# Delta-rule heads on raw keys and queries, decay rows loaded by broadcast, and a fourth weight chunk kept at the end

## The reference, cut to what matters

```
qkv = silu(_dwconv_centred(concat([g_q, g_k, g_v]), gdn_conv_w))       # 5 taps
gq = _l2norm(heads(gq)) * GDN_DK ** -0.5                               # t * rsqrt(sum(t*t) + RMS_EPS)
gk = _l2norm(heads(gk))
gc = cumsum(g, axis=-1)                                                # log decays within a chunk
decay = exp(where(tril, gc[..., :, None] - gc[..., None, :], -inf))
kb = k * beta[..., None]
a = where(strict, kb @ k^T * decay, 0.0) + eye
sol = triangular_solve(a, concat([v * beta, kb * exp(gc)]))            # u, w
attn = q @ k^T * decay;  q_dec = q * exp(gc);  k_dec = k * exp(gc[-1] - gc)
# over the chunks: v_new = u - w @ state;  o = q_dec @ state + attn @ v_new
#                  state = state * exp(gc[-1]) + k_dec^T @ v_new
o = o_f + o_b                                                          # both directions
o = o * rsqrt(mean(o * o) + RMS_EPS) * gdn_norm_w * silu(heads(g_z))
```

## Time and profile before

| what | value |
|---|---|
| median of 3 runs | 1485.69 us (1484.23 to 1486.91) |
| the profiled execution's own time | 1485.09 us |
| its span, first to last instruction | 1483.3 us, mean granted TensorE clock 0.990 |
| TensorE busy | 1417.9 us, 96% |
| VectorE, GpSimd, ScalarE busy | 796.2, 485.3, 462.3 us |
| attention ends, head 0 begins | about 242 us |
| heads 0 to 3 begin their Q projection | 248.7, 350.5, 452.4, 554.2 us |
| the output projection begins | 646.1 us |

### The profile page before, as it was taken

How to read it: one execution, slowest core, us unless ns; L and a number is a source line. 1 busy time by engine, 2 the same in 40 slices (tenths; PEclk the granted TensorE clock), 3 DMA queues, 4 the chain that set the end, 5 groups by cost and what they waited for, 6 DMA issues and landing times.

```text
span 1483.3 us, 19658 instructions
## 1 busy us (share of the span) xinstructions
PE 1417.9 (96%) x7102; PEld 1163.3 (78%) x7102; DVE 796.2 (54%) x1360; ACT 462.3 (31%) x875; POOL 485.3 (33%) x219
## 2 busy tenths in 40 slices
PE   7999999899999899799999999999999999999978
PEld 4877777787787787688878888888888888888866
DVE  4344445976967858952654344344344444225377
ACT  4233345427327346250532222121221222111120
POOL 3322221212121121126454334343443434445460
PEclk9999999999999999999999999999999999999989
DMA  8100100101100100132221111111111114111112
GB/s 244 43 29 29 43 29 15 34 25 33 34 16 29 32 29 23 26 142 78 109 86 42 57 42 46 53 42 57 42 51 48 42 57 184 47 52 43 57 43 99
DMA packets 47207, 82.87 MB, mean 56 GB/s; under 512 B 24240, under 2 KB 26928, under 8 KB 47152
## 3 DMA queue, kind: packets, MB, share of 16 engines
q1 hardware_dynamic: 42400, 66.18, 14.4%
q10 hardware_dynamic: 4752, 15.99, 2.9%
HBM read 72.47 MB, written 9.70 MB: 55 GB/s over the span
## 4 chain that ended last, share of the span: by engine, by line
issue 34%; PE 34%; POOL 15%; DVE 12%; DMA 2%; ACT 1%; POOLq 1%; SPq 0%; DVEq 0%; ACTq 0%
PE banks L600 11%; POOL w_hi L484 8%; POOL w_lo L487 6%; PE banks L947 5%; PE banks L575 3%; PE banks L1047 3%; DVE qkv L1614 2%; PE banks L708 1%; PE banks L730 1%; DVE d_n L1774 1%; PE banks L718 1%; DVE inv L1683 1%; DVE outer L1680 1%; PE banks L923 1%; PE banks L864 1%
## 5 line engine op out<-in xcount | busy, mean ns | idle before, releaser
L484 POOL TENSOR_TENSOR w_hi<-w_raw,one 128x1024 fp32r<-128x1024 f32 (+1 forms) x100 | 190.9, 1909 | 920.6 <-PE banks L575 377.0
L575 PE MATMUL banks<-x_hi,w_hi 128*128 128x512 f32 (+1 forms) x912 | 361.9, 397 | 15.6 <-POOL w_lo L487 10.2
L575 PE MATMUL banks<-x_hi,w_lo 128*128 128x512 f32 (+1 forms) x912 | 356.7, 391 | 0.0
L575 PE MATMUL banks<-x_lo,w_hi 128*128 128x512 f32 (+1 forms) x912 | 356.4, 391 | 0.0
L1902 DVE SCALAR_TENSOR_TENSOR cv<-banks,fw,cv 128x511 f32<-128x511 f32 x176 | 132.0, 750 | 261.7 <-ACT cv L1408 253.9
L487 POOL TENSOR_TENSOR w_lo<-w_raw,w_hi 128x1024 fp32r<-128x1024 f32 (+1 forms) x100 | 255.9, 2559 | 7.8
L575 PEld LDWEIGHTS banks<-x_hi,w_hi 128*128 128x128 f32 (+1 forms) x912 | 171.2, 188 | 54.7 <-POOL w_lo L487 10.2
L575 PEld LDWEIGHTS banks<-x_lo,w_hi 128*128 128x128 f32 (+1 forms) x912 | 171.3, 188 | 38.1 <-issue 2.7
L575 PEld LDWEIGHTS banks<-x_hi,w_lo 128*128 128x128 f32 (+1 forms) x912 | 170.8, 187 | 37.5 <-issue 0.8
L1408 ACT ACTIVATE cv<-banks,fw_j 128x512 f32<-128x512 f32 x88 | 68.5, 778 | 337.3 <-PE banks L575 334.8
L1931 DVE TENSOR_TENSOR a_lo<-act,a_hi 128x1024 fp32r<-128x1024 f32 x44 | 78.4, 1799 | 113.3 <-ACT a_hi L1426 112.9
(11 more groups left out here) (205 smaller groups left out, 1984.8 us busy)
## 6 DMA issues: line engine op xcount, KB each, us to landing
w_raw<-w_all SPq DMA_DIRECT2D x102, 512.0 KB, 3.3
z_tok<-x_tok ACTq DMA_DIRECT2D x8, 512.0 KB, 5.7
x_dram<-z_tok ACTq DMA_DIRECT2D x8, 512.0 KB, 2.6
z<-x_dram ACTq DMA_DIRECT2D x8, 512.0 KB, 7.9
y<-z SPq DMA_DIRECT2D x7, 512.0 KB, 2.6
mix<-xT SPq DMA_DIRECT2D x12, 256.0 KB, 8.5
gb<-ln_row ACTq DMA_DIRECT2D x4, 512.0 KB, 8.4
bw<-rpb SPq DMA_DIRECT2D x8, 132.5 KB, 11.8
```

The costliest lines, as they stand in the source:

```text
L484: nc.gpsimd.tensor_tensor(w_hi[u][:, 0:n], w_raw[ru][:, 0:n], one[:, :].to_broadcast([P, n]), ALU.mult).then_inc(w_high, 1)
L575: last = mm(ps[bank][0:cols, :], w[u][:, k * cols:(k + 1) * cols], seq(x[:, k, :], s), start=n == 0, stop=n == 3 * KT - 1)
```

## The change

It has five parts. (1) **Raw keys and queries.** k and q are no longer normalised. The sums of squares of k come from ScalarE's squares of the turned k (`key_squares`, with the sum of each row), and `key_scales` divides the head's `BETA` and `KAPPA` by them; v is scaled by the length of k while it is turned (`turned_v`). The length of q goes into the output norm: scaled squares of q (`q_sq`) are added to the squares of o by one more product for each half. (2) **Decay rows.** The cumulated log decays are turned once, ahead of attention, copied, and stored to `decay_dram`; for each head `load_decays` spreads the rows over all partitions into `egr`, where `cumulate` put them before. (3) **Order.** `decayed_q` stands behind the first two expansions, k-k products and transposes ahead of Q's second half, GpSimd's first split for the next head waits for `inv_ready`, and the last head's `high_mix(0)` and `low_mix(0)` stand in the state steps. (4) **The end.** `TAIL_CHUNKS` is 4 instead of 3 and `KEPT` 5 instead of 6. (5) Tiles are placed anew.

```diff
-KEPT = 6
-TAIL_CHUNKS = 3
+KEPT = 5
+TAIL_CHUNKS = 4
 # SyncE
             load_chunks(3, GDN0 + 6)
-            with sp.Fori(0, GH) as h:
+            sp.wait_ge(rows_copied, 1)
+            for d in range(2):
+                for hh in range(GH):
+                    rows = decay_rows[d * 4 * NG + hh:(d + 1) * 4 * NG:GH, :]
+                    sp.dma_start(decay_dram[d, hh, :].rearrange("(t n) -> t n", n=P), rows).then_inc(rows_stored, 16)
+            sp.wait_ge(rows_stored, 16 * 2 * GH)
+            def load_decays(h):
+                for d in range(2):
+                    src = decay_dram[d, bass.ds(h, 1), :].to_broadcast([P, T]).rearrange("p (s n) -> p s n", n=L)
+                    sp.dma_start(egr[:, d::2, :], src).then_inc(rows_landed, 16)
+            sp.wait_ge(o_evac, 2 * PAIRS + 1)
+            load_decays(0)
+            def exchange(h, last_head):
...
-                for n in range(6, 10):
+                for n in range(6, 8):
                     load(raw(GDN0 + n), 4 * h + (GDN0 + n))
+                if not last_head:
+                    sp.wait_ge(osum_done, 2 * h + 2)
+                    load_decays(h + 1)
+                for n in range(8, 10):
+                    load(raw(GDN0 + n), 4 * h + (GDN0 + n))
 # GpSimd
-                pool.wait_ge(qd_ready, 4 * h + 4)
+                pool.wait_ge(inv_ready, h + 1)
                 split_later(h, 0)
...
-                if c == CHUNKS - 1:
-                    pool.wait_ge(a_ready, FJ + 2 * KEPT + 2)
+                if c >= CHUNKS - 2:
+                    pool.wait_ge(a_ready, FJ + 2 * KEPT + 2 * (c - CHUNKS + 3))
                 split_one(c, None)
 # TensorE
+            nc.tensor.transpose(ps[4][0:8 * NG, 0:P], gcs[:, 0:8 * NG], ident).then_inc(rows_turned, 1)
...
                 pe.wait_ge(hs_ready, h + 1)
-                for g in range(GROUPS):
-                    cumulate(g)
                 pe.wait_ge(w_ready, c + 2)
                 pe.wait_ge(conv_done, 6 * h + 1)
                 project(0, slot(GDN0 + 1), 0)
-                norm_sum(h, KX, 0)
-                norm_sum(h, KX, 1)
-                pe.wait_ge(conv_done, 6 * h + 2)
-                project(1, slot(GDN0 + 1), 1)
                 for s in range(SEQS):
-                    pe.wait_ge(normed, 4 * h + (s + 1))
+                    pe.wait_ge(silu_done, 6 * h + (s + 1))
...
+                project(1, slot(GDN0 + 1), 1)
                 pe.wait_ge(w_ready, c + 3)
                 pe.wait_ge(conv_done, 6 * h + 3)
                 project(0, slot(GDN0 + 2), 0)
-                cumulated(0)
-                norm_sum(h, QX, 0)
...
-                    mm(ps[2 + s][:, :], mean_w[:, :], q_d[:, s, :], start=True, stop=True).then_inc(osum_done, 1)
+                    mm(ps[2 + s][:, :].rearrange("p (c n) -> p c n", c=CH), mean_w[:, :], q_sq(s), start=True, stop=False)
+                    mm(ps[2 + s][:, :], mean_w[:, :], q_d[:, s, :], start=False, stop=True).then_inc(osum_done, 1)
 # ScalarE
+                def key_squares(s):
+                    act_e.wait_ge(ktr_done, 2 * h + (s + 1))
+                    for cc in range(CH):
+                        n = s * CH + cc
+                        ins = A(x_1[:, s, cc * P:(cc + 1) * P], ps[6 + s][:, cc * P:(cc + 1) * P], ACT.Square,
+                                accum_out=k_sq[:, n:n + 1])
+                    ins.then_inc(k_squared, 1)
...
-                    nc.scalar.copy(vg_tok[:, s, :], ps[7 - s][:, :]).then_inc(vg_tok_ready, 1)
+                    for cc in range(CH):
+                        n = s * CH + cc
+                        ins = A(vg_tok[:, s, cc * P:(cc + 1) * P], ps[7 - s][:, cc * P:(cc + 1) * P], ACT.Copy,
+                                scale=k_norm[:, n:n + 1])
+                    ins.then_inc(vg_tok_ready, 1)
 # VectorE
+                def key_scales():
+                    dve.wait_ge(k_squared, 2 * h + 2)
+                    step(nc.vector.tensor_scalar_add(k_inv[:, :], k_sq[:, :], RMS_EPS))
+                    step(nc.vector.reciprocal(k_inv[:, :], k_inv[:, :]))
+                    scaled = hs[:, BETA * 16:(KAPPA + 1) * 16].rearrange("p (q n) -> p q n", q=4)
+                    step(TT(scaled, scaled, k_inv[:, :].unsqueeze(1).to_broadcast([P, 4, SEQS * CH]), ALU.mult))
...
-                    dve.wait_ge(gc_done, 4 * h + (g + 1))
+                    dve.wait_ge(rows_landed, 32 * h + 32)
...
-                log_decays(0)
-                log_decays(1)
-                normed_x(KX)
-                log_decays(2)
-                log_decays(3)
+                for g in range(GROUPS):
+                    log_decays(g)
                 convolve(h, QX, 0)
+                key_scales()
```

More of the change, by code:

```diff
@@ L154, in encoder_layer @@
             a_lo.append(t)
-        for u in range(2):
+        for u in range(4):
             t, m = place(f"w_tail{4 + u}", [P, D], F32R, m)
@@ L208, in encoder_layer @@
         ecs, at = place("ecs", [P, 2 * 8 * NG], F32, at)
+        decay_rows, at = place("decay_rows", [8 * NG, P], F32, at)
         qkv, at = place("qkv", [P, 3, SEQS, L], F32, mixer)
@@ L230, in encoder_layer @@
         cw, at = place("cw", [P, 3, TAPS], F32, at)
+        k_sq, at = place("k_sq", [P, SEQS * CH], F32, at)
+        k_ln, at = place("k_ln", [P, SEQS * CH], F32, at)
+        k_norm, at = place("k_norm", [P, SEQS * CH], F32, at)
+        k_inv, at = place("k_inv", [P, SEQS * CH], F32, at)
         KX, QX, VX = 0, 1, 2
@@ L253, in encoder_layer @@
         z_tok, _ = place("z_tok", [P, TILES, D], F32, mix0)
-        gb, _ = place("gb", [P, 2, D], F32, first_mix)
+        gb, _ = place("gb", [P, 2, D], F32, early_mix)
         spare_hi, at = place("w_hi3", [P, D], F32R, at)
@@ L375, in unit, with q_sq @@
             return n // BLOCKS, n % BLOCKS
+        def q_sq(s):
+            return d_n[:, :, (1 + s) * P:(2 + s) * P]
         class Chain:
@@ L714, in turn @@
                 pe.wait_ge(p_ready, 8 * pair + (n + 1))
+                if n == 0:
+                    pe.wait_ge(rows_copied, 1)
                 if n >= 2:
@@ L1270, in delta_head @@
                 act_e.wait_ge(head_out, 2 * h + 1)
-                inverse_roots(KX)
+                for s in range(SEQS):
+                    key_squares(s)
                 for g in range(GROUPS):
@@ L1540, in _ @@
                 nc.vector.tensor_scalar_mul(out(NEG_GC), gc, -1.0).then_inc(sc_ready, 1)
-                nc.vector.tensor_copy(out(GLOG), gt_["g"][:, :, hd]).then_inc(sc_ready, 1)
-            dve.wait_ge(sc_ready, 12)
+            dve.wait_ge(sc_ready, 10)
             def biased(pair, n):
@@ L1737, in delta_head @@
                 dve.sem_inc(inv_ready, 1)
-                normed_x(QX)
-                dve.wait_ge(normed, 4 * h + 4)
-                for g in range(GROUPS):
-                    decayed_q(g)
                 convolve(h, VX, 1)
@@ L1756, in delta_head @@
                         expand(packed[:, n:n + CH, :], out(s), done)
+                dve.wait_ge(silu_done, 6 * h + 4)
+                for g in range(GROUPS):
+                    decayed_q(g)
+                dve.wait_ge(qd_ready, 4 * h + 4)
                 for m in range(2):
@@ L1811, in delta_head @@
                                     ALU.mult, ALU.add).then_inc(s_ready, 1)
+                    if last_head and k == 0:
+                        low_mix(0)
                 if not last_head:
```

108 lines of the change are left out of this document (46 added, 62 removed).

## The result

The changed kernel takes **1513.25 us** (median of four runs, 1511.95 to 1514.73), the kernel before 1485.86 on the same chip: a ratio of 1.0186, 95% interval 1.0168 to 1.0203. It is slower, as predicted, but by 27.4 us and not by 9.9, and outside the range. The profiled execution took 1511.95, with a span of 1510.1 us.

What follows compares the result with a forecast made beforehand. A head was taken to last as long as VectorE's list, TensorE counting only where VectorE isn't late. 19 - 4 - 0.3 + 0.2 - 5 = +9.9 on 1485.09 gave 1495.0, predicted as 1496 us; range 1487 to 1505.

Steps and rivals of the forecast that it cites:

- Head 0: First head: decay rows queue on SyncE behind weight loads, so VectorE's log decays wait; +19 us, between +17 and +24.
- rival B: Head 0's decay rows arrive in time, so it gains about 4 like the others: 1473 us; 5%.
- Heads 1 and 2: Middle heads: VectorE's list shortens, the expansion of d_n and the levels come 2.0 us earlier per head; -4 us together.
- Three tiny dependent steps of about 0.2 each: Heads 1 and 2, VectorE: the new key_scales; lower factors still start at 367.7, not 368.19.
- rival D: One stretch per head runs at TensorE's lower clock on the path, up to 2 us each: 1503 us; 10%.
- The last head: Head behind the loop: -3.4 to the levels, +1.2 for low_mix(0), output norm's extra 1.9 uncovered; together -0.3 us.
- the 3.4 forecast: Last head, up to the levels: no loop's turn, and VectorE's 1.30 wait for the norm's roots goes too; -3.4 us.
- The tail: End of kernel: TensorE's last wait is for an a_lo, ending about 1430.5, not 1434.17; -5 us, bounds -3 and -8.
- Rivals A and C: A: TensorE's work bounds the heads, 1478 us, 4%. C: broadcast loads are slow in every head, 1520 us, 6%.

Runs made afterwards that it cites:

- rows_early: The changed kernel with SyncE's decay-row stores and first head's broadcast loads moved ahead of the loads of weight chunks GDN0+4 and GDN0+5: 1486.02 us.
- experiment 4: rows_early with VectorE's loop over the first three heads written out as straight code: 1472.65 us.
- experiment 3: rows_early with 13 further TensorE products per head, results unused, in the two waits ahead of the second level: 1477.90 us.
- Experiment 8: experiment 3's kernel with ten more unused products in the last head: 1477.77 us.
- experiment 10: rows_early with VectorE's loop written out and unused products in all heads (1467.37 us), changed by moving the last head's low_mix(0) one step later: 1462.45 us.
- tail_only: The kernel before with only the tail's change (five kept pairs, four chunks at the end, GpSimd's wait for a_ready): 1478.14 us.

## Why the prediction was wrong

**Head 0 (+19 forecast, +22.7 measured).** The mechanism was right at every link, and within the forecast's bounds. The sizes were off: the split ended 1.2 us later than taken, a store's issue took 0.69 us (5.53 for eight) and not 0.49, which is 1.6 over eight, and from V (288.11) to elimination it took 15.7 and not 14.5. rows_early shows that the stall is SyncE's order and nothing else. It also puts rival B's condition in place, rows in time: but the time is 1486, not that rival's 1473, since what it took for the heads was wrong.

**Heads 1 and 2 (-4 forecast, +4.3 measured): the step that failed.** It read the gain off VectorE's list, as if the list ran on without gaps once its waits were gone. What it foresaw came true: no wait for the rows, loads issued at 371.70 and the decays at 382.04; the wait ahead of the k-q scores gone; a longer wait ahead of V (2.54 us, not 1.14). The waits in the levels came too, but at the second level (2.01 and 1.27) and not at the first, where the prediction looked for them (0.85, before 0.91). Counted from K's first convolution in a head, the expansion of `d_n`, forecast 2.0 us earlier, came 0.3 earlier in head 1 (57.33 against 57.64) and 0.7 later in head 2. Two things were missing:

- *Code.* "Three tiny dependent steps of about 0.2 each" cost 2.06 and 2.17 for the first. The prediction saw the loop's turn only as 3.24 us of cover; experiment 4 shows that it has a second gap, which a VectorE that comes sooner runs into. About +2 in each of the two heads.
- *The clock.* The forecast gave it to rival D with 10%, at up to 2 us in each head, and took the levels to follow the expansion of `d_n` at an unchanged length. It cost 2.6, 1.4 and 2.5 in heads 1 to 3; that it is the clock, experiment 3 shows. The row to ask was at hand: in the earlier trace rows the lower clock already followed a wait of 2.26 us, and the prediction itself put two waits of that size into the levels. D was priced as a rival where the forecast's own waits made it likely.

**The last head (-0.3 forecast, +4.3 measured).** To the levels the head gained 2.6 of the 3.4 forecast. The levels' clock cost 2.5. The way from the last mask to `r` grew by 2.8, where the forecast had 1.2 for `low_mix`: `low_mix` itself puts 1.6 between the copies and `r`, and the copies wait for products at the lower clock. Experiment 8 takes the clock's part away and `r` comes no sooner, as `low_mix` ended 1.1 us behind GpSimd's split either way; experiment 10 moves `low_mix`, and the 2.8 are gone. The output norm cost 1.6 instead of 1.9, rightly seen as uncovered. `low_mix` had its price from the earlier trace rows, where it started ahead of the split; the prediction used the slow price beside GpSimd for the lows of the tail, and not here.

**The tail (-5 forecast, -4.6 measured)**, with the last wait on an `a_lo`: right in mechanism and size, and tail_only bears it out by itself.

**Rivals A and C** did not happen: TensorE's waits for VectorE grew, and the median landing of the broadcast loads was 4.4 us.

The range failed because several losses came on top of one another, each small: 3.5 in head 0, 4 of code, 6.5 of clock and 1.6 of `low_mix` make 15.6 of the 16.9 us by which the sum was short. The rest is within what two executions of one code differ by in a stretch, and stays open.

## What to carry to other kernels

When a wait is taken from an engine that sets the pace, ask what its instructions run into next: code that a loop's turn has not brought yet, a GpSimd that reads SBUF beside them, and a TensorE that now idles in other places and so loses its clock. A transfer that is ready early must also be queued early: here 27 us hung on eight small stores behind one weight load on SyncE. And two limits that lie side by side (here the loop's turn and the normalisation) give next to nothing until both are gone; an edit that measures as no gain may be half of one.

## What the runs showed of the hardware that was not expected

- A wait for code can stand in the trace as the length of an instruction, with no idle before it: 2.06 and 2.17 us for a sum that takes 0.16. The queue of kind "instruction" in the DMA view shows it: one packet in each long sum.
- Products without use made the kernel 8.1 us faster (1486.02 to 1477.90), as they kept TensorE's granted clock at 1.00.
- Four VectorE products of two SBUF inputs took 6.40 us beside a GpSimd split, and 2.50 without it. `low_mix` ended 1.1 us behind a split's end, whether it had started 0.3 or 1.8 us into the split's second half.
